# Attention with the values as weights: split turned probabilities moving, stick-breaking and softmax tiles in pairs by turns

## The reference

```python
logits = q·k * scale + F[t] - F[s]            # s <= t, F = cumsum(log sigmoid(forget logit))
o_fox  = softmax(logits) @ v

z = q·k * scale                               # s < t
log_beta, log_one_minus = log_sigmoid(z), where(mask, log_sigmoid(-z), 0)
after = reverse_cumsum(log_one_minus) - log_one_minus
o_sb  = where(mask, exp(log_beta + after), 0) @ v

o = concatenate([rmsnorm(o_fox) * fox_out_g, rmsnorm(o_sb) * sb_out_g]);  x = x + o @ w_out
```

## Time and profile before

| | |
|---|---|
| median of 3 runs | 2616.19 us (2616.03 to 2618.27) |
| profiled execution | 2616.37 us, span 2614.3 us |
| PE busy | 2563.4 us, 98% of the span |
| DVE, ACT, POOL busy | 53%, 37%, 31% |
| attention rounds | about 1240 to 1787 us |
| PE busy in the last round's 48.5 us | 43.06 us |

### The profile page before, as it was taken

The page is one execution under the profiler, slowest core; times in us unless marked ns, Lnnn a source line. Parts: engine busy times, 40 slices in busy tenths (PEclk is TensorE's granted clock), DMA queues, the critical chain, the costliest instruction groups (busy, mean ns, idle before and its releaser), DMA issues. The chain is left out here.

```text
span 2614.3 us, 32428 instructions
## 1 busy us (share of the span) xinstructions
PE 2563.4 (98%) x12922; PEld 2136.7 (82%) x12922; DVE 1385.5 (53%) x1285; ACT 974.8 (37%) x1376; POOL 820.2 (31%) x339
## 2 busy tenths in 40 slices
PE   8999999999999999999999999999999999999999
PEld 4888888888888888888888888887888888888887
DVE  5864557666666753444735455455764314431454
ACT  3410044434353420023556556563244203321334
POOL 3565443433334335542111011034422222222230
PEclk9999999999999999999999999999999999999999
DMA  8222221212121253342111111131111111111111
GB/s 329 89 87 71 100 88 57 77 52 63 60 81 61 78 199 110 97 145 65 34 41 39 35 41 41 33 125 53 49 48 48 49 48 48 48 49 64 48 57 65
DMA packets 56551, 194.32 MB, mean 74 GB/s; under 512 B 6856, under 2 KB 10824, under 8 KB 55152
## 3 DMA queue, kind: packets, MB, share of 16 engines
q1 hardware_dynamic: 41312, 141.74, 16.6%
q10 hardware_dynamic: 15120, 50.90, 5.6%
HBM read 158.50 MB, written 29.92 MB: 72 GB/s over the span
## 5 line engine op out<-in xcount | busy, mean ns | idle before, releaser
L238 PE MATMUL G<-H_hi,w_hi 128*128 128x512 f32 x1616 | 502.3, 392 | 1.0 <-ACT silu_zB L724 0.7
L269 POOL TENSOR_TENSOR w_lo<-w_raw,w_hi 128x1024 fp32r<-128x1024 f32 x133 | 348.7, 2621 | 491.1 <-ACT w_hi L263 485.3
L238 PE MATMUL G<-H_lo,w_hi 128*128 128x512 f32 x1616 | 497.7, 389 | 0.0
L238 PE MATMUL G<-H_hi,w_lo 128*128 128x512 f32 x1616 | 497.6, 389 | 0.0
L264 POOL TENSOR_TENSOR w_hi<-w_raw,ones 128x1024 fp32r<-128x1024 f32 x75 | 198.2, 2642 | 590.8 <-PE G L238 469.5
L238 PEld LDWEIGHTS G<-H_lo,w_hi 128*128 128x128 f32 x1616 | 303.4, 188 | 63.3
L238 PEld LDWEIGHTS G<-H_hi,w_lo 128*128 128x128 f32 x1616 | 303.4, 188 | 63.2
L238 PEld LDWEIGHTS G<-H_hi,w_hi 128*128 128x128 f32 x1616 | 300.8, 188 | 64.3 <-issue 4.4
L1852 POOL TENSOR_TENSOR w_lo<-w_raw,w_hi 128x1024 fp32r<-128x1024 f32 x24 | 60.2, 2507 | 479.7 <-ACT w_hi L2066 479.7
L1959 PEld LDWEIGHTS G<-att_v,probsT 128*128 128x128 f32 x1152 | 146.5, 191 | 21.9 <-ACT probsT L2095 13.1
L1907 PE MATMUL G<-A_hi,w_hi 128*128 128x512 f32 x368 | 155.7, 423 | 6.6 <-DVE projected L2245 6.3
(11 more groups left out here) (531 smaller groups left out, 4729.4 us busy)
## 6 DMA issues: line engine op xcount, KB each, us to landing
w_raw<-w_in SPq DMA_DIRECT2D x65, 512.0 KB, 3.6
w_raw<-w_up SPq DMA_DIRECT2D x44, 512.0 KB, 3.6
pre_raw<-w_in SPq DMA_DIRECT2D x30, 512.0 KB, 3.6
wm<-w_mod SPq DMA_DIRECT2D x8, 1024.0 KB, 18.5
w_raw<-w_out SPq DMA_DIRECT2D x16, 512.0 KB, 3.7
w_raw<-w_down SPq DMA_DIRECT2D x16, 512.0 KB, 3.6
xT<-xT SPq DMA_DIRECT2D x8, 512.0 KB, 19.3
b_d<-silu_zB ACTq DMA_DIRECT2D x8, 512.0 KB, 2.6
```

Of the source, the lines that this page charges most:

```text
L238: mm = nc.tensor.matmul(dst[:, n * NB:n * NB + c], w[:, k, :], m[:, k, n * NB:n * NB + c], start=first, stop=last)
L269: nc.gpsimd.tensor_tensor(w_lo[:, slot, 0:kt, :], w_raw[:, slot, 0:kt, :], w_hi[:, slot, 0:kt, :].bitcast(F32), ALU.subtract).then_inc(w_r ...
```

## The change

It changes tiles, operands and order in the attention, with the same output.

- **Order of tiles.** Each round has one "s" and one "f" head. Tiles come in pairs of neighbouring query blocks, "s" pair, "f" pair, "s" pair and so on. The columns of `w_in_2`, the gains and the rows of `w_out_2` are ordered for it on the host's layout. The query scale becomes a column `qs` with a sign for each head.
- **Value product.** The values are the weights (`VP`: high parts in 64 columns, low parts in the other 64), the turned probabilities move, 256 columns for a pair of tiles (128 for the last block, which only the second tile has), once their high parts and once their low parts, all in one pass. It runs once for each pair. Its result is the turned output in two halves, which `out half` (ACT) and `out` (DVE) add; `out_turned` is gone.
- **Splitting.** ACT makes `p high` from the bank, DVE `p low`, and the bank is free only after `p low`. `v high` and `v low` likewise, the turned values lying in the upper halves of the score banks.
- **Softmax division.** `made` of an "f" tile is now on DVE: reciprocal of the row's sum, then the whole tile times it.
- **Squares** are taken of the turned outputs and added (`squares added`), and summed over features by 16 one-column products (`heads summed`).
- **Forget sums** are loaded once a round; `rstd1` goes through DRAM and comes back near the end; the early high parts of the outputs are made by ACT, the low parts by GpSimd; eight early tiles instead of seven. `w high` moves to n = 1, 9, 14.

```diff
 def tile_of(g):
-    return X[g // TILES % 2], g % TILES // TT, g % TT
+    u = g % TILES // 2
+    return "sf"[u % 2], u % 2, u // 2 * 2 + g % 2
...
     for c, _, _ in GROUP_AT.get(s, ()):
-        use_u(("p", c), ("act", "p copied", c))
+        use_u(("p", c), ("dve", "p low", c))
...
-def values(g):
+def values(i):
+    g = 2 * i + 1
...
-    for c, b0, n in GROUP_AT[g]:
-        S.wait(pe, "act", "p copied", c)
-        for b in range(n):
-            mm = pe.matmul(V[:, at:at + HD], pT[c % 2][:, b, :], v[:, b0 + b, own_rows(hh)], ...)
+    order = [(b, n) for b in range(tt) for n in range(2)]
+    order = order[:-1] + [(tt, 0), (tt, 1)] + order[-1:]
+    for b, n in order:
+        if b // 4 > arrived:
+            arrived = b // 4
+            S.wait(pe, "dve", "p low", GROUP_AT[g][arrived][0])
+        c0 = P if b == tt else 0
+        mm = pe.matmul(V[:, at + c0:at + 2 * P], VP[:, hh, b, :], pT[n][:, b, c0:2 * P], ...)
...
 PE, step s
-    if s >= 1: values(s - 1)
-    if n == 0 and 1 <= q <= ROUNDS: v_turned(q - 1)
-    if s > TILES and s % TILES == 2: out_turned(s // TILES - 1)
+    if s >= 2 and s % 2 == 0: values(s // 2 - 1)
+    if 0 <= s < STEPS and s % TILES == 0: v_turned(s // TILES)
...
 ACT, step s
     not_taken(nxt)                      # "s" tiles
+    if s >= 5 and s % 4 == 1: out_half(s // 4 - 1)
-    if s >= 1: probs_copied(s - 1)
+    if s >= 1: p_high(s - 1)
+    if s >= 1 and s % TILES == 1: v_high(s // TILES)
+    if s >= 10 and s % 8 == 2: square(s // 8 - 1)
     taken(nxt) or probs(nxt)
...
+    if r == ROUNDS - 1 and 3 <= m < 3 + len(EARLY_TILES):
+        act.wait_ge(o_landed[k], 16)
+        heads_high("heads hi early", k, EARLY_ROWS[k], A[1][:, k, :].bitcast(F32))
...
 DVE, step s (after the evacuations)
+    if 0 <= s + 1 < STEPS: first(s + 1)
+    if s >= 1: p_low(s - 1)
+    if s >= 1 and s % TILES == 1: v_low(s // TILES)
     if s >= 5 and s % 4 == 1: out_of(s // 4 - 1)
+    if s >= 27 and s % 8 == 3: add_squares(s // 8 - 1)
-    if 0 <= s + 1 < STEPS: chain(s + 1)
+    if 0 <= s + 1 < STEPS: made(s + 1)
...
+def made(g):                            # "f" tiles
+    S.wait(v, "act", "exp", g)
+    do("row sum", v.reciprocal(rs[:, n:n + 1], rs[:, n:n + 1]), g)
+    do("made", v.tensor_scalar(p, p, rs[:, n:n + 1], None, ALU.mult), g)
+def p_low(g):
+    for c, b0, n in GROUP_AT[g]:
+        S.wait(v, "act", "p high", c)
+        do("p low", v.tensor_tensor(pT[1][:, b0:b0 + n, cols], blocks_of(bank, n), pT[0][:, b0:b0 + n, cols].bitcast(F32), ALU.subtract), c)
...
 DVE, step 126
     v.wait_ge(x2_landed, 16 * KT)
+    v.wait_ge(r1_landed, 16)
     normed(0); normed(1)
```

More of the change, by code:

```diff
@@ L2001, in _, with part @@
                         piece(q, p)
[L2002 to L2017 removed]
+            values(STEPS // 2 - 1)
+            def part(dst, k, tiles, first, last):
                 for t in tiles:
@@ new lines, in out_of, with add_squares @@
+            def out_of(j):
+                S.wait(v, "act", "out half", j)
+                for hh in range(2):
+                    rows = own_rows(hh)
+                    i = v.tensor_tensor(OT[rows, out_cols(j)], V[rows, 2 * P * hh:2 * P * hh + 2 * P], OT[rows, out_cols(j)], ALU.add)
+                do("out", i, j)
+            def add_squares(i):
+                S.wait(v, "act", "square", i)
+                do("squares added", v.tensor_tensor(SQ[:, square_cols(i)], SQ[:, square_cols(i)], sqt, ALU.add), i)
@@ L2331, in _ @@
             out_of(STEPS // 4 - 1)
-            S.wait(v, "act", "square", TT * ROUNDS - 1)
-            do("heads squares", v.tensor_reduce(ss, ssp.rearrange("p (i x) t -> p x t i", x=2), AX.X, ALU.add))
-            heads_low(LATE, OT)
+            add_squares(2 * ROUNDS - 1)
+            for k, rows in out_rows(ROUNDS - 1):
+                heads_low(k, rows)
             S.wait(v, "act", "heads root")
```

371 lines of the change are left out of this document (192 added, 179 removed).

## The result

The changed kernel takes 2693.39 us (median of 4 runs, 2692.42 to 2696.05) against 2616.11 for the kernel before, timed beside it: ratio 1.0295 [1.0277, 1.0313]. It is 77 us slower. The forecast was 2604 and its range ended at 2640. The profiled execution took 2692.99 us, span 2691.4.

What follows compares the result with a forecast made beforehand. TensorE, busy 98% of the span, was taken as the bound. From 2616.4, seven rounds gave -27 (7.5 saved less 3.7 stall each) and the last round +14.5: about 2604, own range 2592 to 2611, wider range 2578 to 2640.

Steps and rivals of the forecast that it cites:

- Stall 3.7: Added TensorE waits in a main round, 3.7 us, set against 7.5 saved, leaving 3.8 a round, 27 over seven.
- odd half microseconds: Rest of a main round, where a table load stands ahead of a needed copy: 0.5 us of stall.
- tiles 9 to 11: Steps 9 to 11, where k is split: 2.1 us stall plus 0.6 at bank J, 2.7 together.
- tile 5: Step 5, q split: TensorE waits 1.3 us for bank J, 0.8 a round there already, so +0.5.
- the 63.5: TensorE's need in a main round after the change, 71.0 less 7.5 us; VectorE needs 58.9, ScalarE 50.2.
- That is already in the 35.8: GpSimd's stretching of VectorE operations, taken as contained in VectorE's 35.8 us a round before the additions.
- The last round: Last stretch, without projections as cover: 63 us where it took 48.4, so +14.5; bounds +7.5 and +21.
- The tail: From the last value product to the first row's spread: 10 to 12 us, so nothing; bounds -1.5 and +2.
- TensorE's saving: Shorter value product, turned outputs and their bank waits gone: 7.5 us a round, 53 over seven.
- ScalarE's base of 41.2: ScalarE's busy time in a main round before the change, half of each kind of round: 41.2 us.
- The second one: Rival: VectorE's place between copy and bank sets the step; loses from 5.5 us stall a round, 2659 at 11; 0.24 with halfway case.
- The third: Rival: ScalarE sets the step through table changes, each holding it twice 1.28 us: 2630; chance 0.05.

Runs made afterwards that it cites:

- three gone: Changed kernel with Sigmoid for the softmax exponential, no low parts of turned probabilities, and GpSimd's weight low parts for 4 columns only: 2591.54 us, ratio 0.9905.
- one table and no low part: Changed kernel with Sigmoid for the softmax exponential and no low parts of the turned probabilities, their high part used twice: 2611.22 us, ratio 0.9978.
- one table: Changed kernel with Sigmoid in place of the softmax exponential, so ScalarE changes no tables in a round: 2661.33 us, ratio 1.0175.
- small w_lo: GpSimd's low parts of the projection weights for 4 columns only: 2674.21 us against the changed kernel's 2693.39; put in the kernel before, 2614.53.
- kinds by round: Changed kernel with all tiles of a round of one kind, forget sums loaded once in two rounds: 2634.75 us, ratio 1.0068.
- filler: Changed kernel with 16 idle identity transposes before the value product in each step of the last round: 2687.54 us, ratio 1.0270.

## Why the prediction was wrong

**The failed step is "Stall 3.7".** It was the sum of two places walked and 0.5 for everything else. Measured: 76.7 - 63.5 = 13.2 us a round, 66 us over seven rounds beside the forecast. The walk took the copy, the exponential and the bank as free-running and looked at the steps with the most VectorE work; it counted a table load as "odd half microseconds".

The trace says which part of it failed. Laid out by tiles, from the first transpose of one tile to that of the next, as means of the seven rounds, TensorE waits 3.5 us a round at tiles 9 to 11, where the walk had 2.7, and 2.1 at tile 5, where it had 1.3. These two came out near. Everywhere else, put at 0.5, it waits 5.3: 2.2 at tile 3, 1.5 at tile 7, 1.0 at tile 15 and 0.7 at others (at tiles 3 and 5 mostly for the projection bank, at 7, 11 and 15 for the low part). And 4.0 are no waits at all: TensorE is busy 65.7 a round where the 63.5 held 61.7 of work (with three gone it is 62.1, for the same products). Most of that is products that took longer at the lower clock, a term that the forecast did not have. The removals put 4 to 5 of these 13.2 on the tables, about 5 on the low part, 2 to 3 on GpSimd beside VectorE, and 2 on the rest.

**One wait was not in the walk at all**: the half output, which now stands in ScalarE's queue ahead of the next copy and needs the value product that needs the low part. ScalarE waited 80.2 us there, longer than for anything else. It closes the ring in the piece of the chain shown above. That a table load moved ahead of it wins 11 us fits this; no run moves the half output itself, so what it costs is not shown.

**"That is already in the 35.8"** was wrong for GpSimd's low parts. Before, they stretched three operations in each stick-breaking round (a 256-column scan, a 1024-column scan and the low part of k) and none in a softmax round: 12 operations, 22 us over the seven rounds. Now they stretch three in every round: 21 operations, 35 us. Their removal gives 19 us instead of 3.

**The last round**: 63 was forecast, 79.6 came, though VectorE was busy 54.9 (forecast 56) and ScalarE 47.3 (forecast 55). So 16 us more of waiting, and the same failure. Its low part alone is 18.3. With one table and no low part it is still 60.2, and small w_lo changes nothing there. From the first transpose of the last round, the kernel with three gone takes 59.7 where the kernel before takes 40.9. The early high parts are not it (2.4 us), and the filler gave 3.7. Two suspects stand in the traces, and no run takes either away alone: the scans, which the kernel before does not have in its last round ("kinds by round" removes them together with the tables), and GpSimd's low parts of the outputs, beside which VectorE loses 9.2 us in the changed kernel and 12.1 in the one with three gone. How the remaining 19 divide stays open.

**The tail** was put at nothing, with bounds up to +2, and cost 4.6. From the last value product to the spread of the first row it takes 14.8 us, where 10 to 12 were forecast and 11.7 measured before. The chain of its waits answers to the earlier trace rows:

```profile
1859.65 4.11 PE G L2018 x18
1863.76 3.97 PE S L2029 x32
1867.73 6.75 PE G L2018 x18
1874.48 1.72 PE S L1809 x4
```

The 16 column sums (two records each) take 4.0 us, not 2 to 3, and stand on the path between the products. The second 18 products take 6.75 us where the first took 4.11: for most of them the clock was at its lower level, and they start 0.43 us apart instead of 0.23.

```profile
1867.70:1874.50 6.80, 6.80 (x20) 5.39 (x20) 2.61 (x3) 0.27 (x1) 0.00 (x0) 0.62 0.00 0
```

So 2.6 us of the tail's loss are the clock, behind a round in which TensorE waited much.

**Right**: the new product's 0.12 us; TensorE's saving (the round of 65.4 with the three gone); VectorE's and ScalarE's busy times within 1.1 and 1.6 us a round, VectorE's in part by luck (by the two kernels with small w_lo the stretching grew from 3.1 to 5.0 a round, so its own work is 52.8 where 55.8 was forecast, and in the last round 54.9 holds 9.2 of stretching); a table load's 1.28 us with the activation 1.29 after its start; TensorE's waits led by the low part, but 6.2 us a round and 4.0 for the bank J, not 3 in all. ScalarE's base of 41.2 is 40.2 by the two windows of the earlier trace rows and 41.3 by the seven rounds, which changes nothing.

**The rivals.** The second one's condition was met, and its direction: above 5.5 us of stall a round the change loses. Its price was too small even at its far end (11 a round, 2659), and its mechanism is only half true: the low part on VectorE is late, but not through its place behind the scan. Moving it ahead lost 10 us more. The third had the right culprit for 32 us by another path: no load lasted longer than its row, and each was paid at its place. The advice of the Trainium skill ("ScalarE: Activation LUTs", Table sets: the hidden batching unit) to batch activations by table set held: with one table the kernel is 32 us faster. The drain that the Trainium skill ("ScalarE: Activation LUTs", What ACT_TABLE_LOAD costs) adds to each load stands in no row here. TensorE's clock, 0.67 in the last stretch and 0.96 in the rounds, stood nowhere in the forecast; the filler gave 5.9 us back, and 2.6 show in the tail.

The reading behind all of it: the busy share, as a mean over a round, was taken as the test. VectorE at 93% of the step was called tight and then given 3.7 us. The kernel before already loses 0.59 of the table changes put behind its copy, in both kinds of round; it loses the low part only where VectorE then has 61 of 79 us to do, 0.6 of its length there and none in the softmax rounds. The changed kernel gets back 0.37 to 0.58 of what is taken away; the division alone cost nothing. ScalarE need not be near full for a loss; for VectorE the share in the round concerned told in that experiment, and the mean of two unlike rounds did not.

## What to carry to other kernels

Work put on a ring of in-order queues cost 0.34 to 0.59 of its length here in five cases, as a mean over the rounds, on engines that idle a quarter to a half of the time. It cost nothing in a sixth (the division) and little in a seventh (GpSimd's stretching in the kernel before). Before making such a change, put the suspected instruction into the kernel that exists, at its place, and time that, round by round. It tells the sign sooner than the size: 62, 26 and 3 us here for the 32, 48 and 19 in the changed kernel. Walk the whole ring of a step, each queue in its order, and ask of every new wait what stands behind it; busy shares tell only whether the engine could be the bound by itself, and only over stretches that are alike. When removals add up to what they give together, stop looking for one culprit.

## What the runs showed of the hardware

- A VectorE scan or product with SBUF operands beside a 2.5 us GpSimd subtraction takes 1.2 to 2.0 us longer in these kernels: the scan of 256 columns 2.70 us for 0.69 in each of the changed kernel's seven rounds, that of 768 columns 3.35 to 3.71 for 1.76, the 1024-column product 2.42 to 3.18 for 1.22. Operations that read the turned probabilities' bank are not stretched: the low part of 512 columns takes 0.67 us beside GpSimd and 0.68 without.
- An activation table load is 1.28 us and the activation follows 0.01 us behind it; 63 of them took 81 us in this stretch, and without them the kernel is 32 us faster.
- 256-column products of this type start 0.12 us apart, where the old product took 0.216 us a block, in two records of 64 columns.
- The granted clock fell to the lower of its two levels (1.2 of 2.4 GHz) for parts of stretches in which TensorE waited: mean 0.67 over a stretch where it was busy 45 of 80 us, 0.91 with idle transposes added, 1.00 in the rounds of the kernel with three gone, where it was busy 435 of 458.
